# The low halves of the weights made on VectorE, in its own order of steps, instead of on GpSimd

## What is computed

```python
for l in range(DEPTH):
    u = rmsnorm(h, norm_g[l])
    p = u @ w_in[l]
    hq, hf_f, hf_b, hi, hgt, aq, ak, av, agt = jnp.split(p, split_idx, axis=-1)
    o_h = hgrn2_mixer(hq, hf_f, hf_b, hi, hgt, lbs[l], hg_norm_g[l])
    o_a = diff_attention_mixer(aq, ak, av, agt, diff_lambda[l], diff_subln_g[l], l, cos, sin)
    h = h + jnp.concatenate([o_h, o_a], axis=-1) @ w_out[l]
out = rmsnorm(h, final_norm_g)[:, N_META:]
```

## Time and profile before

| | us |
|---|---|
| median of three runs | 1586.7 |
| lowest and highest | 1586.59, 1586.84 |
| the profiled execution's own time | 1587.14 |
| its span in the profile | 1585.3 |
| TensorE busy (matmul) | 1496.3 (94%) |
| VectorE busy | 986.5 (62%) |
| ScalarE busy | 772.8 (49%) |
| GpSimd busy | 533.2 (34%) |

### The profile page before, as it was taken

How to read it: one execution, slowest core, us unless ns; L and a number is a source line. 1 busy time by engine, 2 the same in 40 slices (tenths; PEclk the granted TensorE clock), 3 DMA queues, 4 the chain that set the end, 5 groups by cost and what they waited for, 6 DMA issues and landing times.

```text
span 1585.3 us, 27727 instructions
## 1 busy us (share of the span) xinstructions
PE 1496.3 (94%) x11148; PEld 1412.5 (89%) x11148; DVE 986.5 (62%) x1542; ACT 772.8 (49%) x1689; POOL 533.2 (34%) x287
## 2 busy tenths in 40 slices
PE   5999999999999999999979999999999999999986
PEld 4999999999999999998879999999998898888874
DVE  6666677676734666666465666676676356665655
ACT  5445444554434555555434544445444345565542
POOL 2323322333333333333333333333333343333331
PEclk8999999999999999999989999999999999999999
DMA  4221111211223222222122121221212232222221
GB/s 155 81 67 55 54 58 63 68 55 54 68 68 94 68 68 68 67 65 66 59 67 75 60 67 54 67 63 58 68 54 67 67 96 79 67 71 78 74 62 66
DMA packets 34480, 109.39 MB, mean 69 GB/s; under 512 B 4912, under 2 KB 5040, under 8 KB 34352
## 3 DMA queue, kind: packets, MB, share of 16 engines
q1 hardware_dynamic: 34352, 107.61, 21.9%
HBM read 96.84 MB, written 2.10 MB: 62 GB/s over the span
## 4 chain that ended last, share of the span: by engine, by line
PE 76%; DVE 13%; issue 6%; ACT 2%; DMA 1%; POOL 1%; SPq 1%; DVEq 0%; ACTq 0%; POOLq 0%
PE proj L1247 51%; PE pair L1316 7%; PE meta L1426 3%; PE pair L1411 2%; PE pair L1413 2%; PE main L1440 2%; DVE stage L969 1%; PE main L1381 1%; DVE totals L1030 1%; PE main L1382 1%; DMA q_stack<-gate_f 1%; PE pair L1362 1%; DVE neg_max L1160 1%; DVE o_rows L1104 1%; PE main L1323 1%
## 5 line engine op out<-in xcount | busy, mean ns | idle before, releaser
L509 POOL TENSOR_TENSOR w_lo<-w_raw,w_hi 128x1024 fp32r<-128x1024 f32 x178 | 441.9, 2484 | 753.9 <-ACT w_hi L568 752.1
L1247 PE MATMUL proj<-u_hi,w_hi 128*128 128x264 f32 (+1 forms) x2048 | 497.0, 314 | 15.2 <-DVE u_lo L923 15.2
L1247 PE MATMUL proj<-u_hi,w_lo 128*128 128x264 f32 (+1 forms) x2048 | 466.8, 300 | 0.0
L1247 PE MATMUL proj<-u_lo,w_hi 128*128 128x264 f32 (+1 forms) x2048 | 466.8, 299 | 0.0
L1247 PEld LDWEIGHTS proj<-u_hi,w_hi 128*128 128x128 f32 x2048 | 329.4, 191 | 27.9 <-issue 16.3
L1247 PEld LDWEIGHTS proj<-u_hi,w_lo 128*128 128x128 f32 x2048 | 327.3, 189 | 11.1
L1247 PEld LDWEIGHTS proj<-u_lo,w_hi 128*128 128x128 f32 x2048 | 327.9, 190 | 7.6
L1160 DVE TENSOR_REDUCE neg_max<-pair 128x1 f32<-128x528 f32 (+1 forms) x144 | 101.3, 704 | 226.7 <-PE pair L1413 226.6
L743 ACT ACTIVATE decay<-pair,neg_max 128x528 f32<-128x528 f32 (+1 forms) x144 | 100.7, 699 | 253.9 <-DVE neg_max L1160 253.9
L568 ACT ACTIVATE w_hi<-w_raw 128x1024 fp32r<-128x1024 f32 x178 | 186.6, 1049 | 22.2 <-DMA w_raw<-w_units 11.9
L689 ACT ACTIVATE qk_dec<-ops 128x528 f32<-128x528 f32 (+1 forms) x112 | 75.8, 677 | 126.1 <-DVE ops L1057 126.1
(11 more groups left out here) (182 smaller groups left out, 2253.4 us busy)
## 6 DMA issues: line engine op xcount, KB each, us to landing
w_raw<-w_units SPq DMA_DIRECT2D x178, 512.0 KB, 3.5
k_stack<-k_stack SPq DMA_DIRECT2D x32, 132.0 KB, 2.3
q_stack<-gate_f SPq DMA_DIRECT2D x32, 132.0 KB, 2.4
h<-x_t SPq DMA_DIRECT2D x8, 264.0 KB, 4.7
out_t<-decay SPq DMA_DIRECT2D x4, 256.0 KB, 2.1
out_t<-ops SPq DMA_DIRECT2D x4, 256.0 KB, 2.1
cos_sin<-rope SPq DMA_DIRECT2D x1, 528.0 KB, 5.5
masks<-level_masks SPq DMA_DIRECT2D x1, 448.0 KB, 5.3
```

Source lines behind the costliest of these rows:

```text
L509: pool.tensor_tensor(w_lo[:, u % N_CUT, :, :], w_raw[:, u % N_RAW, :, :], w_hi[:, u % N_CUT, :, :].bitcast(f32), ALU.subtract)\
L1247: ins = pe.matmul(out, w, x[:, k, cols_n], start=(k == 0 and p == 0), stop=(k == last_k and p == 2))
```

## The change

GpSimd's `cut_low` goes, and GpSimd keeps `cut_mixed` and `invert_rms` alone. VectorE gets a `cut_low` with the same operation on the same buffers and the same two semaphores. Where it stands in VectorE's order: unit 0 ahead of the first norm, units 1 and 2 inside it; then the low half of unit i + 3 after the `follow` of unit i in the dense stretches (start and end of a layer), and inside the heads in the step after the one in which ScalarE makes the high half (`units_cut`). In HGRN heads those are mostly the steps 1, 4, 7, 9 and 12, in attention heads the steps 1, 4, 7 and 11. `cut_mixed(n - 1)` on GpSimd now stands ahead of `invert_rms(n)` with nothing between.

```diff
--- before.py
+++ after.py
@@ -189,6 +189,14 @@
 def units_left(c):
 
     return units_after(c, steps_of(c)) if c >= 0 else ()
+
+
+def units_cut(c, s):
+
+    if s == 0:
+        return units_after(c - 1, steps_of(c - 1) - 1) if c > 0 else ()
+    earlier = units_left(c - 1) if s == 1 else ()
+    return [*earlier, *(units_after(c, s - 1) if c < HEADS else ())]
 
 
 def units_followed(c, s):
@@ -504,12 +512,6 @@
             pool.memset(o_rows[:, N_CHUNKS, :], 0.0).then_inc(pads_set, 1)
             pool.memset(k_low[:, :, :].bitcast(f32), 0.0).then_inc(pads_set, 1)
 
-            def cut_low(u):
-                pool.wait_ge(hi_cut, u + 1)
-                pool.tensor_tensor(w_lo[:, u % N_CUT, :, :], w_raw[:, u % N_RAW, :, :],
-                                   w_hi[:, u % N_CUT, :, :].bitcast(f32), ALU.subtract)\
-                    .then_inc(lo_cut, 1)
-
             def invert_rms(n):
 
                 pool.wait_ge(sq_ready, n + 1)
@@ -528,27 +530,13 @@
                                    mix_hi[:, n % 8, ts].bitcast(f32), ALU.subtract)\
                     .then_inc(mix_lo_ready, 1)
 
-            for u in range(N_CUT):
-                cut_low(u)
             for l in range(DEPTH):
-                base = l * LAYER_UNITS
-
-                def follow(units):
-                    for i in units:
-                        if base + i + N_CUT < DEPTH * LAYER_UNITS:
-                            cut_low(base + i + N_CUT)
-
-                follow(range(len(HG_TILES)))
                 for c in range(HEADS):
                     n = l * HEADS + c
-                    for s in range(steps_of(c)):
-                        if s == mix_step(c) and c > 0:
-                            cut_mixed(n - 1)
-                        follow(units_after(c, s))
+                    if c > 0:
+                        cut_mixed(n - 1)
                     invert_rms(n)
-                    follow(units_left(c))
                 cut_mixed(l * HEADS + HEADS - 1)
-                follow(range(OUT_LATE, LAYER_UNITS))
 
 
         @block.scalar
@@ -895,6 +883,18 @@
                 w = step(dve.tensor_scalar(g_final[:, :], g_final[:, :], math.sqrt(D_MODEL), None, ALU.mult))
                 after(w)
 
+            def cut_low(u):
+
+                dve.wait_ge(hi_cut, u + 1)
+                dve.tensor_tensor(w_lo[:, u % N_CUT, :, :], w_raw[:, u % N_RAW, :, :],
+                                  w_hi[:, u % N_CUT, :, :].bitcast(f32), ALU.subtract).then_inc(lo_cut, 1)
+
+            def cut_after(l, units):
+
+                for i in units:
+                    if l * LAYER_UNITS + i + N_CUT < DEPTH * LAYER_UNITS:
+                        cut_low(l * LAYER_UNITS + i + N_CUT)
+
             def add_squares(n, k):
 
                 dve.wait_ge(h_sq, n * KT + k + 1)
@@ -917,6 +917,8 @@
                         dve.scalar_tensor_tensor(qk_dec[:, (k % 4) // 2, k % 2, :], h[:, k, :],
                                                  g_in[:, l, k:k + 1], sq[:, :], ALU.mult, ALU.mult)\
                             .then_inc(u_ready, 1)
+                    if l == 0 and k in (2, 4):
+                        cut_low(k // 2)
                     if k > 0:
                         j = k - 1
                         dve.wait_ge(u_hi_ready, l * KT + j + 1)
@@ -1195,28 +1197,35 @@
             for k in range(KT):
                 dve.wait_ge(x_in[k], 16)
             after(step(dve.tensor_scalar(g_in[:, :, :], g_in[:, :, :], math.sqrt(D_MODEL), None, ALU.mult)))
+            cut_low(0)
             for l in range(DEPTH):
                 norm_u(l)
                 if l == 0:
                     prepare_lower_bounds()
                 for i in range(len(HG_TILES) - 1):
                     follow(l, i)
+                    cut_after(l, [i])
                 for c in range(HEADS):
                     for s in range(steps_of(c)):
                         (hgrn if c < HG_HEADS else attend)(l, c, s)
                         if c == 0 and s == 1:
                             follow(l, len(HG_TILES) - 1)
+                            cut_after(l, [len(HG_TILES) - 1])
                         if s == stack_step(c) + 1 and HG_HEADS <= c + 1 < HEADS:
                             stack_low(l * AT_HEADS + c + 1 - HG_HEADS)
                         for i in units_followed(c, s):
                             follow(l, i)
+                        cut_after(l, units_cut(c, s))
                 scale_output(l * HEADS + HEADS - 1)
                 for i in units_not_followed(HEADS - 1):
                     follow(l, i)
+                cut_after(l, units_cut(HEADS, 0))
+                cut_after(l, units_cut(HEADS, 1))
                 gate_main(l, HEADS - 1)
                 gate_meta(l, HEADS - 1)
                 for i in range(OUT_LATE, LAYER_UNITS):
                     follow(l, i)
+                    cut_after(l, [i])
                     if i > OUT_C:
                         add_squares(l + 1, TILE_ORDER.index(UNITS[i][2]) - 1)
             norm_out()
```

## The result

| | before | after |
|---|---|---|
| median of four executions, us | 1586.7 | 1562.6 (1561.6 to 1563.0) |
| span of the profiled execution, us | 1585.3 | 1560.7 |
| granted clock, mean | 0.988 | 0.994 |

What follows compares the result with a forecast made beforehand. TensorE, busy 94% of the span, was taken to set the time. The terms -5.8 - 8.6 - 5.2 - 2.7 + 5.4 - 0.9 - 1.0 sum to -18.8 us from 1587.1, forecast 1568, range 1559 to 1580.

Steps and rivals of the forecast that it cites:

- From head 7 to 8: Way from head 7 to 8: a rotary product ahead of TensorE's 2.56 us wait is no longer held; -2.7 us for two.
- HGRN heads: Gated-recurrence heads, both layers: step 4's cut replaces a hold, so all TensorE waits of 1.1 and 4.7 us go; -5.8 us.
- the cover in step 12: HGRN heads: VectorE waits for ScalarE's high half, but the next head's start operands keep 2.0 us of cover; costs nothing.
- Attention, layer 1: Attention heads of layer 1: a 1.7 us hold gives way to a 1.15 us cut; -4.1 us over five heads.
- Layer 0: Attention heads of layer 0: step 7's hold gives way to a shorter cut, step 1's waits go whole; -8.6 us.
- Head 8: Head 8, both layers: cuts come late behind VectorE's other work, so TensorE waits 1.1 and 1.6 us; +5.4 us.
- Between the layers: Between the layers: the last sum of squares stands behind a cut and ScalarE's high half; +3.6 us, +1.7 for the part.
- Start: Kernel start: second scaled tile no longer held, first projection at 21.3 instead of 23.33, but a cut between the u_lo; -1.0 us.
- (a): Rival, all gaps: they get another owner, such as ScalarE's copies or the q_stack copy; half the gain, 1577 us; chance 0.20.
- (b): Rival, VectorE's cuts: each costs 2.4 us as on GpSimd; 26 us over the forecast, 1594; chance 0.07 shared with (c).
- (c): Rival, VectorE: stretching is not GpSimd's doing and stays, cuts come on top; 24 us more, 1611; chance 0.07 shared with (b).
- (d): Rival: VectorE's lead closes twelve remaining 0.4 us waits and hides head 8's 5.4 us; 10 us more gain, 1558; chance 0.10.

Runs made afterwards that it cites:

- pool_reads: Changed kernel, with GpSimd also doing an unused subtraction of the same size, reading SBUF, where its 178 low halves stood: 1653.8 us.
- pool_writes: Changed kernel, with GpSimd doing three memsets of a scratch tile, which read nothing, where its 178 low halves stood: 1564.3 us.
- tail_cut_late: Changed kernel, with step 7's low half on VectorE moved behind step 8's work in attention heads 9 to 14 of each layer: 1553.8 us.
- head8_early: Changed kernel, with VectorE's low halves ahead of the step's own attention work in steps 0 to 3 of head 8 only: 1556.1 us.
- start_order: Changed kernel, with the second tile's high half ahead of ScalarE's first root and its low half right behind the first low half: 1560.8 us.
- cut_doubled: Changed kernel, with a second, unused subtraction of the same size ahead of each of VectorE's 178 low halves: 1628.4 us.
- head8_first: Changed kernel, with VectorE's low halves ahead of the step's own attention work in all steps of head 8 of each layer: 1559.7 us.

## Why the prediction was right, and where its sizes were off

**The mechanism.** GpSimd's low halves held VectorE's products of two SBUF operands, and the change takes the holder away: shown by the pair `pool_reads` and `pool_writes`. The cut's price was taken at 1.23 us from a shorter instruction of its kind, and is 1.22. VectorE's busy time is 1006.7 us, at the low end of the range given (1000 to 1100).

**What the sum left out.** The forecast added up waits, and the idle time fell by 17.5 us where it had 18.8. The busy time of the matmuls had no term, and it fell by 7.1. Without that the time would have come out near the forecast, but by parts that err both ways; the largest of them is next.

**From head 7 to 8: -2.7 forecast, -3.2 measured, and the agreement is luck.** The hold went and the waits of 2.56 us and, in layer 1, 2.65 are 1.21 and 1.27, as reckoned. But the waits of 0.71 and 1.44 us for the copy of `q_stack` opened behind them, so that the idle time of the two stretches fell by 0.6 us only. The other 2.6 us came from the clock: before, the long wait was followed by matmuls at a granted clock of 0.50, and the shorter one is not. The same stretch of TensorE's work, of head 7 in layer 0, from the second row behind the wait on, before and after (columns as under `tail_cut_late`: window, length, busy us and instructions of the five engines, clock, DMA share, GB/s):

```profile
411.56:413.69 2.13, 2.13 (x12) 2.13 (x11) 2.07 (x3) 1.11 (x2) 0.92 (x1) 0.50 0.21 48
```

```profile
407.52:409.53 2.01, 2.01 (x20) 2.01 (x19) 1.98 (x3) 1.36 (x3) 0.52 (x1) 1.00 0.04 8
```

In 2.13 us TensorE did 12 matmuls, in 2.01 us now 20.

**HGRN heads: -5.8 forecast, -8.0 measured.** The waits went, the cover in step 12 held. The step that was off in size is the reading of a wait's price off its idle row. In layer 1 a head took 43.35 us and takes 42.41, 0.94 less, for an idle time of 43.35 - 42.68 = 0.67; the other 0.27 was in the busy time of the same matmuls. These rows, of the kernel before and of the changed one, are the same head:

```profile
1012.23:1055.58 43.35, 42.68 (x313) 40.34 (x312) 29.31 (x45) 20.86 (x43) 14.80 (x8) 1.00 0.19 62
```

```profile
1000.21:1042.62 42.41, 42.41 (x313) 40.26 (x312) 28.58 (x50) 20.88 (x43) 2.73 (x3) 1.00 0.19 63
```

**Attention, layer 1: -4.1 forecast, -7.2 measured**, in part by the same term. A head went from 37.05 us to 35.78; its idle time fell from 1.70 to 0.83 us (the wait for the combined maps from 1.22 to 0.68, that of 0.30 went), and the busy time of the same matmuls by 0.40. That makes 1.3 us in five heads, where 0.8 were counted, and 0.7 in a sixth that was not counted: 2.2 us of the 7.2 are busy time. **Layer 0: -8.6 and -8.0.** The wait left in step 8 was forecast at 0.4 us and is 0.41; the idle time fell by 7.2.

**Head 8: +5.4 and +7.0.** The two waits were forecast at 1.1 and 1.6 us and are 1.12 and 1.69, at the pieces named; the head grows by 3.5 and not by 2.8, the rest is busy time again. That they were the cause is shown by `head8_early`, which takes 6.6 of the 7.0 away.

**Between the layers.** The wait for the sum of squares was forecast at "near 5" and is 4.93, 3.51 more than before. The window nevertheless got 0.5 us shorter, and not 1.7 longer. In it lie, beside the waits counted here, those of the last attention head and of the first recurrent one, which the forecast had in other terms (0.68 us of one, 1.31 of another are gone). The long wait and the slower matmuls behind it were made good there in part by a shorter slow stretch at the start of the second layer: 13 pairs of matmuls at the slow pace before, 8 after. The forecast had no term for that. The end: -3.7 and -4.3.

**Start: -1.0 and -0.4.** The first projection begins at 21.28 as forecast (21.3), but the cut between the two `u_lo` made a wait of 0.68 us, and fifteen pairs of matmuls ran at the slow pace where eleven had before. By `start_order` this order costs 1.7 us and not 1.0.

**Sum.** Of the 5.8 us by which the gain was larger, 2.2 are in HGRN heads, 3.1 in attention of layer 1, 2.2 between the layers, 0.6 at the end, 0.5 from head 7 to 8, less 1.6 in head 8, 0.6 in attention of layer 0 and 0.6 at the start.

**The rivals.** (a), half the gain: it fell as a whole, but in one place it is what happened, on the way to head 8, where the copy of `q_stack` took over 0.71 and 1.44 us; ScalarE's copies did not take over a gap in the attention heads. (b), a cut of 2.4 us: it fell with the 1219 ns; its price was set at +26, and `cut_doubled` measured +66 for 1.2 us more on every cut, since attention heads have two places each and not one, and the way from head 7 to 8, counted at nothing, has one (+7.9); 25 of the 66 us are busy time, which no price of a place contained. Its break-even of 2.0 us a cut is not settled. A straight line between the two kernels, an estimate, gives 1.22 + 24.1 / 66 x 1.22 = 1.67 us, but a longer cut costs little at first and more later (19.7 us for 0.93 below 1.22, 66 for 1.22 above it); at the first of these rates it would be 1.22 + 24.1 / 19.7 x 0.93 = 2.36 us, so it lies somewhere between. (c), load alone: it fell, but a kernel with both the load on VectorE and the reads on GpSimd takes 1653.8 us and not 1611. (d), a larger gain by hiding the twelve waits of step 8 and head 8's: not by this change; `tail_cut_late` and `head8_early` hide them, for 8.8 and 6.5 us.

## What to carry to other kernels

GpSimd subtracting from SBUF and VectorE working on two SBUF operands did not run side by side here: before GpSimd is counted as free, look whether stretched VectorE instructions end where its own do. Where work goes onto an engine that feeds the bottleneck, its place in the order counts for more than its amount: here 217 us of subtractions cost 22 us more in nearly right places than in better ones, and 64 more still where they wait for their own input. The price of a wait was 1.25 to 1.5 times its idle time in the heads read here, and more where the granted clock fell to its lower level behind it; so idle and busy time of the bottleneck are worth accounting for apart. And the slack has to be listed for every step, since once it is used up a further microsecond on every cut costs two and a half times as much (66 us for 1.22 against 19.7 for 0.93).

## What the runs showed of the hardware that was not expected

- The holding isn't bound to two operands. With memsets on GpSimd, VectorE's one-operand scaling has a median of 1146 ns, and 435 without; the two-operand product in front of it isn't touched (VectorE, then GpSimd, in `pool_writes`):

```profile
201.93 0.28 DVE L1060 TENSOR_TENSOR totals<-totals 128x132 f32<-128x132 f32 x1
202.13 0.68 DVE L999 TENSOR_SCALAR stage<-stage,one_minus_lb,lb 128x528 f32<-128x528 f32 x1
202.84 1.15 DVE L1001 TENSOR_SCALAR gate_f<-stage 128x528 f32<-128x528 f32 x1
...
201.57 3.31 POOL L544 MEMSET scratch<- 128x1024 f32 x3 [4.95 <-ACT w_hi L584]
```

  The same section of the Trainium skill counts such scalings among the instructions that can take VectorE's second pair of ports in a faster mode and then contend with any GpSimd instruction; 435 ns for 528 columns, against 704 for a product, and the memsets' effect agree.
- VectorE's row maximum, which reads PSUM, was never lengthened: 144 of them lie between 687 and 710 ns in `pool_reads`, where products of two SBUF operands reach 2437.
- GpSimd is held by VectorE in its turn, it seems by whichever began first. Its subtraction takes 1.89 us in many places of `pool_reads` and 2.93 in others. In the first pair of rows GpSimd began first and VectorE is stretched; in the second VectorE's cut began 0.04 us ahead and GpSimd takes 1.04 us longer:

```profile
112.45 1.89 POOL L543 TENSOR_TENSOR scratch<-ones 128x1024 fp32r<-128x1024 f32 x1 [5.06 <-ACT w_hi L583]
112.78 1.71 DVE L1059 TENSOR_TENSOR totals<-totals 128x132 f32<-128x132 f32 x1
...
104.41 1.23 DVE L916 TENSOR_TENSOR w_lo<-w_raw,w_hi 128x1024 fp32r<-128x1024 f32 x1
104.45 2.93 POOL L543 TENSOR_TENSOR scratch<-ones 128x1024 fp32r<-128x1024 f32 x1 [1.18 <-ACT w_hi L583]
```

- A wait raises TensorE's busy time of the same matmuls at a full granted clock, by 0.16 us for an idle time of 0.38 and by 0.27 for one of 0.67. What of it is the restart of the stream and what the way in which ends are modelled stays open.
- Behind some waits the granted clock goes to its lower level. It is 0.50 behind the waits of 2.56 and 2.65 us in the kernel before, of 2.18 in `head8_first` and of 2.86 in head 8 of `cut_doubled` (444.10 to 447.30). It stays at 1.00 behind the waits of 1.21 and 1.27 that took the place of the first two, and also behind one of 2.95 in `cut_doubled` (418.40 to 421.40), so that the length of the wait alone does not decide it.
